# Low-rank norms moved into the projections and the Fourier part, rotary products moved ahead in the up-projections

## The reference

```python
def rms_norm(x, g):
    y = x * lax.rsqrt(jnp.mean(x * x, axis=-1, keepdims=True) + EPS)
    return y * g

p  = modulate(x, norm1_g, sh1, sc1) @ w_in        # 512 tokens
pc = modulate(ctx, norm1_g, csh1, csc1) @ w_in    # 256 context tokens
cq  = rms_norm(p[..., O_CQ:O_CKV], q_norm_g)      # 256 wide
q   = cq @ w_uq                                   # 4 heads x (128 nope + 64 rope)
ckv = rms_norm(p[..., O_CKV:O_KR], kv_norm_g)     # 128 wide, the same for pc
kv  = ckv @ w_ukv                                 # 4 heads x (128 key + 128 value)
k_pe, q_pe = apply_rope(p[..., O_KR:O_HQ]), apply_rope(q[..., 128:])
attn = softmax attention of q over keys and values of tokens and context
fn   = fourier_mix(p[..., O_FN:IN_WIDTH], w_fourier)
hg   = gated linear scan (hgrn2)
y    = concat([attn, hg, fn]) @ w_out
```

## Time and profile before

| what | value |
|---|---|
| median of 3 runs | 2618.89 us (2617.77 to 2621.63) |
| profiled execution, its own time | 2617.71 us |
| its span in the trace | 2615.9 us |
| PE busy | 2396.8 us (92%) |
| DVE busy | 1005.6 us (38%) |
| ACT busy | 728.1 us (28%) |
| POOL busy | 235.5 us (9%) |
| TensorE clock granted, mean | 0.934 of full |

### The profile page before, as it was taken

How to read it: one execution, slowest core, us unless ns; L and a number is a source line. 1 busy time by engine, 2 the same in 40 slices (tenths; PEclk the granted TensorE clock), 3 DMA queues, 4 the chain that set the end, 5 groups by cost and what they waited for, 6 DMA issues and landing times. The chain is left out here.

```text
span 2615.9 us, 32465 instructions
## 1 busy us (share of the span) xinstructions
PE 2396.8 (92%) x13850; PEld 1829.3 (70%) x13850; DVE 1005.6 (38%) x1577; ACT 728.1 (28%) x1234; POOL 235.5 (9%) x255
## 2 busy tenths in 40 slices
PE   6978999988999999996689999999987997999997
PEld 3535556776888877885667888887865555788885
DVE  2013118534333326745223433423335663442333
ACT  2123200123222223313222332422103563342331
POOL 0003107400000000003000000000021441000000
PEclk8989999999999998987569999998996998999999
DMA  7020004311223122100011222212210003222210
GB/s 295 37 84 33 33 32 153 138 65 65 81 87 122 73 74 97 65 33 2 4 65 65 97 97 97 97 68 97 97 35 1 1 2 129 96 97 97 97 65 33
DMA packets 17119, 196.35 MB, mean 75 GB/s; under 512 B 2000, under 2 KB 3152, under 8 KB 5072
## 3 DMA queue, kind: packets, MB, share of 16 engines
q1 hardware_dynamic: 15824, 189.67, 19.4%
q10 hardware_dynamic: 1152, 4.61, 0.4%
HBM read 190.08 MB, written 2.10 MB: 73 GB/s over the span
## 5 line engine op out<-in xcount | busy, mean ns | idle before, releaser
L1585 DVE TENSOR_TENSOR wsp_mlp<-ring,wsp_mlp 128x1024 fp32r<-128x1024 f32 x128 | 156.9, 1226 | 437.5 <-ACT wsp_mlp L1547 437.5
L1547 ACT CAST wsp_mlp<-ring 128x1024 fp32r<-128x1024 f32 x128 | 134.3, 1049 | 348.7 <-PE psum L1532 344.2
L1529 PE MATMUL psum<-hs_mlp,wsp_mlp 128*128 128x512 f32 x512 | 201.3, 393 | 8.1 <-DVE hs_mlp L1418 8.1
L1529 PE MATMUL psum<-acts_mlp,wsp_mlp 128*128 128x512 f32 x512 | 202.4, 395 | 0.0
L1531 PE MATMUL psum<-hs_mlp,wsp_mlp 128*128 128x512 f32 x512 | 200.9, 392 | 0.0
L1532 PE MATMUL psum<-hs_mlp,wsp_mlp 128*128 128x512 f32 x512 | 200.8, 392 | 0.0
L1532 PE MATMUL psum<-acts_mlp,wsp_mlp 128*128 128x512 f32 x512 | 199.4, 389 | 0.0
L1531 PE MATMUL psum<-acts_mlp,wsp_mlp 128*128 128x512 f32 x512 | 199.3, 389 | 0.0
L1585 DVE TENSOR_TENSOR wsp_ffn<-ring,wsp_ffn 128x1024 fp32r<-128x1024 f32 x66 | 80.9, 1226 | 236.5 <-ACT wsp_ffn L1547 236.5
L424 PE MATMUL psum<-hsev,wspev 128*128 128x512 f32 x672 | 158.1, 398 | 3.9 <-DVE wspev L404 3.9
L424 PEld LDWEIGHTS psum<-hsev,wspev 128*128 128x128 f32 x672 | 129.6, 193 | 32.1 <-DVE wspev L404 4.7
(11 more groups left out here) (423 smaller groups left out, 4120.8 us busy)
## 6 DMA issues: line engine op xcount, KB each, us to landing
ring<-weights SPq DMA_DIRECT2D x85, 2048.0 KB, 8.0
ring<-weights SPq DMA_DIRECT2D x3, 1024.0 KB, 4.9
cst<-consts ACTq DMA_DIRECT2D x1, 2209.0 KB, 15.0
xT<-xin SPq DMA_DIRECT2D x2, 1024.0 KB, 6.6
ring<-weights SPq DMA_DIRECT2D x1, 1280.0 KB, 6.1
mixT<-ctxin ACTq DMA_DIRECT2D x1, 1024.0 KB, 14.9
ring<-weights SPq DMA_DIRECT2D x2, 512.0 KB, 3.3
arena<-arena_low SPq DMA_DIRECT2D x8, 128.0 KB, 2.3
```

Source lines behind the costliest of these rows:

```text
L1529: pe.matmul(tile_bank(g, j), w_hi, src[:, 0, k0 + i, :], start=(first and i == 0), stop=False)
L1547: act.copy(wsp[:, q % 2, 0, :], raw_view(q)).then_inc(s["w_hi"], 1)
L1585: dve.tensor_tensor(wsp[:, q % 2, 1, :], raw_view(q), wsp[:, q % 2, 0, :].bitcast(F32), ALU.subtract).then_inc(s["w_lo"], 1)
```

## The change

The two norm blocks are gone. Their operations go elsewhere: the squares (ACT) and the sums by the ones matrix (PE) into the projections, the square roots (ACT), reciprocals and scaling (DVE) into the Fourier part. The sums of `cq` go to bank 6, those of `ckv` to bank 7 (tokens) and bank 3 (context); the Fourier part's eight outputs share the other five banks, by `F_BANK`. The reciprocal is now written over the square root. In the up-projections `kpe_raw` is turned before the first output, `qp` 0 and `qp` 1 ahead of outputs 7 and 9. Nothing in the number of operations changes but this: the norm of `ckv` was one operation over 768 columns for square, root, reciprocal and scaling, and is now one over 512 and one over 256; its matmuls were two already.

```diff
@@ -699,7 +699,8 @@
         cqT = sb("cqT", [P, 2, T], s1)
         ckvT = sb("ckvT", [P, 1, TA], s1)
         kpe_raw = sb("kpe_raw", [P, TA], s1)
-        tile_done, tile_out = sem("tile_done"), sem("tile_out")
+        tile_done, tile_out, low_squares, low_summed = (
+            sem(n) for n in ("tile_done", "tile_out", "low_squares", "low_summed"))
         with nc.Block() as block:
             @block.tensor
             def _(pe):
@@ -731,6 +732,11 @@
                     last = product(pe, bank(4 + j), lambda k: w[:, k, j * P:(j + 1) * P], lambda k: hT[:, k, :], KD)
                     last.then_inc(tile_done, 1)
                 used(tile_done, 14)
+                pe.wait_ge(tile_out, 12)
+                pe.wait_ge(low_squares, 4)
+                product(pe, bank(6), lambda k: C("ones"), lambda k: mixT[:, k, :], 2).then_inc(low_summed, 1)
+                pe.matmul(bank(7), C("ones"), mixT[:, 2, :], start=True, stop=True).then_inc(low_summed, 1)
+                pe.matmul(bank(3, TC), C("ones"), mixT[:, 3, 0:TC], start=True, stop=True).then_inc(low_summed, 1)
 
             @block.scalar
             def _(act):
@@ -749,6 +755,10 @@
                     n += 1
                     act.wait_ge(tile_done, n)
                     act.copy(dst, bank(b, TC)).then_inc(tile_out, 1)
+                act.wait_ge(tile_out, 12)
+                for dst, raw in ((mixT[:, 0, :], cqT[:, 0, :]), (mixT[:, 1, :], cqT[:, 1, :]),
+                                 (mixT[:, 2, :], ckvT[:, 0, 0:T]), (mixT[:, 3, 0:TC], ckvT[:, 0, T:TA])):
+                    act.activation(dst, raw, ACT.Square).then_inc(low_squares, 1)
                 for j in range(2):
                     n += 1
                     act.wait_ge(tile_done, n)
@@ -764,33 +774,50 @@
         fa = sb("fa", [P, 2, 2, T], s3)
         fm = sb("fm", [P, 2, T], s3)
         f_done, f_out = sem("f_done"), sem("f_out")
+        low_root, low_inv = sem("low_root"), sem("low_inv")
+        F_BANK = (0, 1, 2, 4, 5, 0, 1, 2)
+        low_norms = ((bank(6), QL, ((cqT[:, 0, :], V("q_norm_g", 0, 1)), (cqT[:, 1, :], V("q_norm_g", 1, 1)))),
+                     (bank(7), KVL, ((ckvT[:, 0, 0:T], V("kv_norm_g")),)),
+                     (bank(3, TC), KVL, ((ckvT[:, 0, T:TA], V("kv_norm_g")),)))
         with nc.Block() as block:
             @block.tensor
             def _(pe):
                 w = take(pe, "dft").rearrange("p (f k n) -> p f k n", f=2, k=TT)
                 for f in range(2):
                     for j in range(2):
-                        last = product(pe, bank(2 * f + j), lambda k: fn_tok[:, k, j * P:(j + 1) * P],
+                        last = product(pe, bank(F_BANK[2 * f + j]), lambda k: fn_tok[:, k, j * P:(j + 1) * P],
                                        lambda k: w[:, f, k, :], TT)
                         last.then_inc(f_done, 1)
                 used(f_done, 4)
                 pe.wait_ge(f_out, 4)
                 for j in range(2):
-                    pe.matmul(bank(4 + j), C("dft_cos64"), fa[:, 0, j, :], start=True, stop=False)
-                    pe.matmul(bank(4 + j), C("dft_nsin64"), fa[:, 1, j, :], start=False, stop=True).then_inc(f_done, 1)
+                    out = bank(F_BANK[4 + j])
+                    pe.matmul(out, C("dft_cos64"), fa[:, 0, j, :], start=True, stop=False)
+                    pe.matmul(out, C("dft_nsin64"), fa[:, 1, j, :], start=False, stop=True).then_inc(f_done, 1)
                 pe.wait_ge(f_out, 6)
                 w = take(pe, "fourier")[:, 0:512].rearrange("p (k n) -> p k n", k=2)
                 for j in range(2):
-                    last = product(pe, bank(6 + j), lambda k: w[:, k, j * P:(j + 1) * P], lambda k: fm[:, k, :], 2)
+                    last = product(pe, bank(F_BANK[6 + j]), lambda k: w[:, k, j * P:(j + 1) * P], lambda k: fm[:, k, :], 2)
                     last.then_inc(f_done, 1)
                 used(f_done, 8)
 
             @block.scalar
             def _(act):
+                for sums_of, width, _ in low_norms:
+                    act.activation(sums_of, sums_of, ACT.Sqrt, bias=epsc[:, 0:1], scale=1.0 / width).then_inc(low_root, 1)
                 for n in range(8):
                     act.wait_ge(f_done, n + 1)
                     dst = fa[:, n // 2, n % 2, :] if n < 4 else fm[:, n - 4, :] if n < 6 else mixT[:, n, :]
-                    act.copy(dst, bank(n)).then_inc(f_out, 1)
+                    act.copy(dst, bank(F_BANK[n])).then_inc(f_out, 1)
+
+            @block.vector
+            def _(dve):
+                for e, (root, _, tiles) in enumerate(low_norms):
+                    dve.wait_ge(low_root, e + 1)
+                    dve.reciprocal(root, root).then_inc(low_inv, 1)
+                    dve.wait_ge(low_inv, e + 1)
+                    for x, gain in tiles:
+                        dve.scalar_tensor_tensor(out=x, in0=x, scalar=gain, in1=root, op0=ALU.mult, op1=ALU.mult)
 
             @block.sync
             def _(sync):
@@ -799,9 +826,6 @@
         s2.close()
 
 
-        norm(cqT, mixT, cqT, 2, TT, 1.0 / QL, lambda k: V("q_norm_g", k, 1))
-        sqk = mixT[:, 0:2, :].rearrange("p (o a) n -> p o (a n)", o=1)
-        norm(ckvT, sqk, ckvT, 1, TAT, 1.0 / KVL, lambda k: V("kv_norm_g", k, 1))
         s4 = ExitStack()
         qn = mixT[:, 0:4, :]
         qp = sb("qp", [P, 2, T], s4)
@@ -813,15 +837,24 @@
             outs = [(T, qp[:, j, :]) for j in range(2)] + [(T, qn[:, h, :]) for h in range(MH)]
             outs += [(n, kn[:, h, a:a + n]) for h in range(MH) for a, n in ((0, T), (T, TC))]
             outs += [(512, v_mla[:, i, :]) for i in range(TAT)]
+            turned = (kpe_raw[:, 0:T], qp[:, 0, :], qp[:, 1, :])
 
             @block.tensor
             def _(pe):
                 ch = take(pe, "mla_up")
                 wq = ch[:, 0:2 * 768].rearrange("p (k n) -> p k n", k=2)
                 wkv = ch[:, 2 * 768:2 * 768 + 1024]
+                def rotate(e):
+                    if e == 2:
+                        pe.wait_ge(roped, 1)
+                    pe.matmul(bank(6 + e % 2), C("rot_mla"), turned[e], start=True, stop=True).then_inc(rot_done, 1)
+
+                rotate(0)
                 for n, (width, _) in enumerate(outs):
                     if n >= 6:
                         pe.wait_ge(t_out, n - 5)
+                    if n in (7, 9):
+                        rotate((n - 5) // 2)
                     out = bank(n % 6, width)
                     if n < 6:
                         c0 = (512 + n * P) if n < 2 else (n - 2) * P
@@ -835,12 +868,6 @@
                         last = pe.matmul(out, ckvT[:, 0, i * P:(i + 1) * P], wkv[:, 512:1024], start=True, stop=True)
                     last.then_inc(t_done, 1)
                 used(t_done, len(outs))
-                for r in range(3):
-                    if r == 2:
-                        pe.wait_ge(roped, 1)
-                    src = qp[:, r, :] if r < 2 else kpe_raw[:, 0:T]
-                    pe.wait_ge(t_out, 2)
-                    pe.matmul(bank(6 + r % 2), C("rot_mla"), src, start=True, stop=True).then_inc(rot_done, 1)
 
             @block.scalar
             def _(act):
@@ -854,8 +881,7 @@
             @block.vector
             def _(dve):
                 link = chain(dve, "rope_chain")
-                for r in range(3):
-                    x = qp[:, r, :] if r < 2 else kpe_raw[:, 0:T]
+                for r, x in enumerate(turned):
                     dve.wait_ge(rot_done, r + 1)
                     link(dve.tensor_tensor(bank(6 + r % 2), bank(6 + r % 2), C("sin_mla"), ALU.mult))
                     link(dve.tensor_tensor(x, x, C("cos_mla"), ALU.mult))
```

## The result

Measured against the kernel before in alternation, the changed kernel takes 0.9941 of its time, 95% interval 0.9913 to 0.9968: 15.5 us less, between 8 and 23. The medians of the five runs each are 2604.0 and 2621.6 us, 17.6 apart. Timed again later with new runs of both, the ratio was 0.9909 (0.9884 to 0.9934), 24 us less. Over all runs of the study the mean of the changed kernel is 2600.4 us (13 runs, standard deviation 4.8), of the kernel before 2621.3 us (61 runs, standard deviation 6.6): **20.9 us less, give or take some 3**. The forecast was 26.2 less with a time of 2587 to 2599. The direction is right; the gain is smaller than forecast, and 2604.0 lies outside the range, as does the mean of all 13 runs, 2600.4.

What follows compares the result with a forecast made beforehand. PE, busy 92% of the span, was taken as the bound, losing time where it stands still or runs at half clock. Terms -19.6 + 2.4 - 3.95 - 2.6 - 2.4 = -26.2 us took the median from 2618.9 to 2592.7; range 2587 to 2599.

Steps and rivals of the forecast that it cites:

- The norms: Between Fourier part and up-projections: the 19.9 us of norm work shrink to one barrier of 0.32, -19.6 us.
- the sums: End of the projections: four ones-matmuls cost 3.0 us but cover the last Silu, net +2.4 us.
- the rotary products: Between up-projections and first score: 6.85 us shrink to 0.32, three products add 2.6, net -3.95 us.
- the clock at the up-projections: First 24 up-projection records run at full clock, 10.3 us where they took 12.88: -2.6 us.
- The cover: Fourier part: DVE's 10.9 us of reciprocals and scaling cost 0, with 10 us of cover in a 23.4 us stage.
- The clock in attention: First eight score records of attention run at full clock, 2.85 us where they took 5.26: -2.4 us.
- behind which eight records took 2.85 us, full clock: Attention: the 2.97 us rest before 216.40 was followed by full clock, so both half-clock stretches should go.
- or falls elsewhere for as long: Rival on the clock terms: no clock gain, or an equally long fall elsewhere, 5.0 us more, 2597.7; chance 9%.
- Everything later lies 26 us earlier: Sign of being right: in the new profile all that follows attention's start moves 26 us earlier.
- the shift rival: Later half-clock stretches, as in the second block, end sooner or later: 2587 to 2589 or 2596 to 2600; chance 9%.
- The norm work: Rival: norm work surfaces under the Fourier part, 2593 if DVE takes twice its time, 2604 at three times; chance 2%.
- attention did not stay at half clock: Rival: attention's stage runs at half clock, up to 66 us more, 2659, slower than before; chance 1%.

Runs made afterwards that it cites:

- rotary_only: Kernel before with only the rotary products moved as in the change, both norm blocks kept; 0.9960 of the time of the kernel before.
- warm_attn: Changed kernel plus three unread matmuls filling PE's 2.97 us rest before attention's second scores; 0.9898 of the time of the kernel before.

## Why the prediction was right and wrong

**The norms, the sums, the rotary products: right.** Their terms with the clock at the up-projections add up to -19.6 + 2.4 - 3.95 - 2.6 = -23.75 us to the first score. Measured are 23.4 in the first pair of traces and 24.0 between the means of five and four (160.3 and 136.3). By part: -19.6 to -19.9 with only the norms moved (forecast, without the rotary term, -19.8), and -3.6 to -3.9 with only the rotary products (-3.95). The cover held as costed: 11.1 us of DVE work for 10.9, over 10 us before the stage ends. The barrier behind the sums was 0.32 us, not 0.92, as chosen.

**The clock in attention: half wrong.** The step "behind which eight records took 2.85 us, full clock" read the 2.97 us rest as harmless, though one of 3.26 us before the first scores went with the half clock there. It was harmless in all traces of before, and in `rotary_only` as well. In all four traces of the changed kernel the clock fell 7.6 to 8.4 us behind the first score, just after that rest, and took back 1.6 of the 2.6 us that `rotary_only` and `warm_attn` gained in attention; attention to readout went from 298.4 to 297.5, where 2.4 less were forecast. The rival "or falls elsewhere for as long" had named such a fall, with 9% and at 5.0 us. Filling the rest showed that the fall needs it; why the same rest did no harm in the other kernels stays open.

**"Everything later lies 26 us earlier": this is the step that failed.** The forecast took one execution as it stood and held the rest of the program for constant, so the readout stage had no term in the sum, nor in its bounds but for 3 us. The first trace of before was one with the short readout (29.5 us), the first of the changed kernel one with the long (36.8). By the means of all traces the readout cost before 32.5 us and the changed kernel 35.0; that difference of 2.5 rests on five and four draws, and its size stays open. With it the account is -24.0 - 0.9 + 2.5 = -22.4, against -20.9, give or take 3, in the timed runs. With the readout's fall removed on both sides, the change is worth 2593.5 - 2616.7 = -23.2 us, give or take 4 (the two kernels ran in different series, with before at 2621.4 and 2620.6), and from the first projection to the readout's norm 464.2 against 488.3, -24.1 (one trace each). The Trainium skill's rule that was set against the sum ("TensorE: Matmul & The Clock Gate", Part 1), that the point of change varies from run to run, is what these traces show: in the five of before the readout's fall came 0.0, 0.0, 0.0, 0.3 and 0.5 us into the stage. The forecast gave this 9% and no term.

Set against the forecast median of 2592.7, the mean of 2600.4 is 7.7 us too long. Of this 2.4 is the base, as said below, and 1.5 attention (-0.9 for -2.4). Of the 3.8 left the readout's 2.5 may be a part; the runs' spread of some 3 us doesn't let more be said.

**The range: too narrow**, since it took the executions' spread from three runs (3.9 us). 61 runs of the same kernel lie between 2608.7 and 2634.5, and the mean of the changed kernel, 2600.4, lies at the end of what the shift rival had given 9%, 2596 to 2600. The term "2587 to 2589, or 2596 to 2600" with 9% should have been most of the range's width. The base was off as well: before's mean is 2621.3, not 2618.9.

**The rivals.** The norm work did not surface under the Fourier part, and attention did not stay at half clock: 63 us from 197 on at 1.00.

```profile
192.00:197.00 5.00, 4.60 (x10) 2.25 (x12) 0.16 (x1) 0.35 (x2) 4.15 (x2) 0.66 0.01 3
197.00:260.00 63.00, 59.85 (x378) 43.52 (x379) 20.42 (x44) 24.89 (x51) 30.70 (x14) 1.00 0.00 1
```

But the state that it feared, small matmuls at half clock while PE is busy, came in the readout instead: 16.8 of the first 17.0 us busy, at 0.53. It made 7.4 us, not 66.

## What to carry to other kernels

Cost a change in its own stretch and check it there: from the first projection to the first score the five traces of before repeat within 1.3 us, while whole executions differ by 26. Not every stretch repeats so: the readout's two lengths lie 7.4 us apart, and only several traces show both. Before forecasting a total, ask for the spread over many runs, and list the places where PE changes clock; each can be a draw of some microseconds that a single profile shows as if it were fixed. Where PE rests for a microsecond or three ahead of a stage of narrow matmuls, a few wide ones that nobody reads can be worth more than they cost: six of them brought the changed kernel from 2600.4 (13 runs) to 2591.4 us (6 runs) in the mean, and those six executions within some 5 us of each other.

## What the runs showed of the hardware that was not expected

The clock can stay down while PE works nearly all the time: 17.1 us in eight traces of the readout. In the changed kernel's trace that is the stretch

```profile
482.50:499.50 17.00, 16.78 (x83) 16.41 (x84) 5.39 (x20) 3.36 (x5) 0.00 (x0) 0.53 0.23 96
```

with matmuls of 64 and 128 columns. At the up-projections of before, with 512 columns, the clock was back about 5 us after PE's start. The two stretches differ in more than width, and no run varied width alone, so what kept the clock down isn't shown. With the three wide matmuls ahead of it the same stage ran at full clock.

And the same rest of 2.97 us, in the same place, was followed by a fall in all four traces of the changed kernel and in none of the five of before. In before the clock had risen some 5 us before the second scores; but in `rotary_only` it had been full for 29 us and didn't fall either, so a recent rise isn't what protects it.

The clock's changes kept their distance from each other and not from the program: the fall at the readout came 453.97 us behind the rise in the first projections in five traces of before out of five, while the program stood up to 1.7 us differently against that rise.
